# Value stage of an expert feed-forward: six sums kept in their PSUM banks over all 128 blocks instead of being added out every four blocks

## The reference, cut to what matters

```
def per_head(hargs):
    e, g = hargs
    act = jax.nn.gelu(jnp.einsum('ld,lkd->lk', xb, u_tab[e]), approximate=False)
    return jnp.einsum('lk,lkd->ld', act * g, v_tab[e])
...
    y = peer_ffn(h, peer_wq[l], peer_keys[l], peer_u[l], peer_v[l])
    h = layer_norm(DEEPNORM_ALPHA * h + y, ln2_g[l], ln2_b[l])
```

## Time and profile before

| What | us |
| --- | --- |
| median of three runs | 2871.51 (2864.45 to 2873.06) |
| the profiled execution's own time | 2873.07 |
| its span, first to last instruction | 2871.3 |
| first `ex_gated_hi` to last `ex_gated_hi` of the value stage | 582.12 |
| last `ex_gated_hi` to the first instruction of the layer norm | 19.31 |
| mean granted TensorE clock over the span | 0.949 of full |

### The profile page before, as it was taken

How to read it: one execution, slowest core, us unless ns; L and a number is a source line. 1 busy time by engine, 2 the same in 40 slices (tenths; PEclk the granted TensorE clock), 3 DMA queues, 4 the chain that set the end, 5 groups by cost and what they waited for, 6 DMA issues and landing times. The chain is left out here.

```text
span 2871.3 us, 43150 instructions
## 1 busy us (share of the span) xinstructions
PE 2503.2 (87%) x14285; PEld 1409.1 (49%) x14285; DVE 1771.6 (62%) x3539; ACT 900.6 (31%) x1357; POOL 1232.4 (43%) x744
## 2 busy tenths in 40 slices
PE   5999998967999999988989899978888698888885
PEld 3344343435677766675434455545555233333332
DVE  6123122027676666753331798889997688888886
ACT  4212212123323333222223333334443233333332
POOL 3312313213122122212323577666565576777764
PEclk9999999988999999999989999999999899999998
DMA  5201201121000000002231588768989899999994
GB/s 184 88 29 58 88 29 66 52 84 45 8 29 22 29 29 29 7 0 85 78 126 49 166 266 285 246 223 314 350 325 354 280 310 310 315 317 316 315 312 144
DMA packets 192978, 456.84 MB, mean 159 GB/s; under 512 B 17664, under 2 KB 100224, under 8 KB 192784
## 3 DMA queue, kind: packets, MB, share of 16 engines
q1 hardware_dynamic: 149136, 296.59, 29.6%
q0 software_dynamic: 36864, 134.23, 14.6%
q10 hardware_dynamic: 6912, 25.17, 2.2%
HBM read 403.50 MB, written 52.43 MB: 159 GB/s over the span
## 5 line engine op out<-in xcount | busy, mean ns | idle before, releaser
L1760 POOL TENSOR_TENSOR hid_u_lo<-hid_u,hid_u_hi 128x1024 bf16<-128x1024 f32 x128 | 292.9, 2289 | 228.8 <-ACT hid_u_hi L1744 228.4
L2373 PE MATMUL bank<-ex_v_hi,ex_gated_hi 128*128 128x512 bf16 x768 | 301.4, 392 | 85.4 <-DVE ex_gated_lo L2431 73.4
L148 PE MATMUL bank<-hT_hi,hid_u_hi 128*128 128x384 bf16 x1024 | 337.6, 330 | 39.2 <-POOL hid_u_lo L1760 28.3
L2411 POOL TENSOR_TENSOR ex_v_lo<-ex_v,ex_v_hi 128x1024 bf16<-128x1024 f32 x128 | 274.3, 2143 | 153.8 <-ACT ex_v_hi L2395 153.7
L148 PE MATMUL bank<-hT_lo,hid_u_hi 128*128 128x384 bf16 x1024 | 337.2, 329 | 0.0
L148 PE MATMUL bank<-hT_hi,hid_u_lo 128*128 128x384 bf16 x1024 | 336.9, 329 | 0.0
L203 POOL TENSOR_TENSOR ret_w_lo<-ret_w_raw,ret_w_hi 128x1024 bf16<-128x1024 f32 x72 | 153.0, 2162 | 401.4 <-ACT ret_w_hi L198 401.4
L2373 PE MATMUL bank<-ex_v_hi,ex_gated_lo 128*128 128x512 bf16 x768 | 300.3, 391 | 0.0
L2373 PE MATMUL bank<-ex_v_lo,ex_gated_hi 128*128 128x512 bf16 x768 | 299.3, 390 | 0.0
L2438 DVE SCALAR_TENSOR_TENSOR wide<-ex_row,row_gated,wide 128x1024 f32<-128x1024 f32 x128 | 164.4, 1284 | 17.2 <-DMA ex_row<-in_peer_v,row_index 16.9
L2397 ACT ACTIVATE ex_gated_hi<-ex_gated 128x384 bf16<-128x384 f32 x128 | 66.9, 522 | 343.0 <-DVE ex_gated L2428 343.0
(11 more groups left out here) (486 smaller groups left out, 5785.7 us busy)
## 6 DMA issues: line engine op xcount, KB each, us to landing
hid_u<-in_peer_u SPq DMA_DIRECT2D x128, 512.0 KB, 5.5
ex_v<-in_peer_v SPq DMA_DIRECT2D x128, 512.0 KB, 6.1
ret_w_raw<-in_w_ret SPq DMA_DIRECT2D x60, 512.0 KB, 4.2
expert_hidden<-hid_gelu SPq DMA_DIRECT2D x128, 192.0 KB, 4.5
expert_weights<-spread_grid ACTq DMA_DIRECT2D x48, 512.0 KB
ex_gated<-expert_hidden SPq DMA_DIRECT2D x128, 192.0 KB, 4.6
ex_weights<-expert_weights SPq DMA_DIRECT2D x64, 384.0 KB, 5.8
dn_w_raw<-in_w_dn SPq DMA_DIRECT2D x36, 512.0 KB, 3.3
```

The source lines that it names most:

```text
L148: last = nc.tensor.matmul(out, left[l], right[r], start=start and i == 0, stop=stop and i == len(PASSES) - 1)
L1760: self.nc.gpsimd.tensor_tensor(self.us[1][:, m % 2, :, :], self.u32[:, m % RING, :, :], self.us[0][:, m % 2, :, :], ALU.subtract).then_inc ...
L2373: last = nc.tensor.matmul(bank[:, :], gs[l][:, slot, t * P:(t + 1) * P], vs[r][:, slot, half * 512:(half + 1) * 512], start=j == 0 and i == 0,
L2411: nc.gpsimd.tensor_tensor(vs[1][:, n % 8, :], v32[:, n % RING, :], vs[0][:, n % 8, :], ALU.subtract).then_inc(s["v_lo"], 1)
```

## The change: what it does

The groups go. Each of the six units has its bank for the whole stage: PE takes block after block, all six units of a block with three matmuls each, and adds up in the banks from block 0 (`start`) to block 127 (`stop`). DVE no longer adds out of PSUM inside the stage. At the end it does one operation per unit that scales `h` by ALPHA and adds the bank, so the six scalings ahead of the stage go too. The bf16 halves keep eight slots, now a plain ring: ACT waits before `ex_v_hi` of block n until PE is through with block n - 8 (`used`). Loads, gathers, the products, the splits and the row additions are unchanged, in the same order on their engines.

```
-            for j in range(GROUP):
-                step(j, j, None)
-            with eng.Fori(0, (BLOCKS - 2 * GROUP) // (2 * GROUP)) as turn:
-                for j in range(2 * GROUP):
-                    step(turn * (2 * GROUP) + (GROUP + j), GROUP + j, turn * 2 + j // GROUP)
...
+            for n in range(SLOTS):
+                step(n, n)
+            with eng.Fori(0, (BLOCKS - 2 * SLOTS) // SLOTS) as turn:
+                for j in range(SLOTS):
+                    step(turn * SLOTS + (SLOTS + j), SLOTS + j)
+            for n in range(BLOCKS - SLOTS, BLOCKS):
+                step(n, n)
...
             @block.tensor
             def _(pe):
-                def units(n, m, group):
-
-                    side = (m // GROUP - 1) % 2
-                    for u in units_of(m):
...
-                        pe.wait_ge(s["added"], group * UNITS + (u + 1))
-                        for j in range(GROUP):
-                            slot = GROUP * side + j
-                            for i, (l, r) in enumerate(PASSES):
...
+                def step(n, m):
+                    first, last_one = isinstance(n, int) and n == 0, isinstance(n, int) and n == BLOCKS - 1
+                    slot = m % SLOTS
+                    for name in ("gated_hi", "gated_lo", "v_hi", "v_lo"):
+                        pe.wait_ge(s[name], n + 1)
+                    for u, (half, t) in enumerate(UNITS):
+                        for i, (l, r) in enumerate(PASSES):
+                            last = nc.tensor.matmul(core.banks[u][:, :], gs[l][:, slot, t * P:(t + 1) * P],
+                                                    vs[r][:, slot, half * 512:(half + 1) * 512],
+                                                    start=first and i == 0, stop=last_one and i == 2)
+                        if last_one:
+                            last.then_inc(s["summed"], 1)
+                    if not last_one:
+                        last.then_inc(s["used"], 1)
...
             @block.scalar
...
-                    if m >= GROUP:
-
-                        act.wait_ge(s["added"], group * UNITS + UNITS)
+                    if m >= SLOTS:
+
+                        act.wait_ge(s["used"], n - (SLOTS - 1))
...
             @block.vector
             def _(dve):
-                def add_units(n, m, group):
-                    for u in units_of(m):
-                        half, t = divmod(u, TILES_IN)
-                        dve.wait_ge(s["unit"], group * UNITS + (u + 1))
-                        part = acc[:, t, half * 512:(half + 1) * 512]
-                        nc.vector.tensor_tensor(part, part, core.banks[u][:, :], ALU.add)\
-                            .then_inc(s["added"], 1)
...
-                    if m >= GROUP:
-                        add_units(n, m, group)
...
-                for u in range(UNITS):
-                    half, t = divmod(u, TILES_IN)
-                    part = acc[:, t, half * 512:(half + 1) * 512]
-                    nc.vector.tensor_scalar(part, part, ALPHA, None, ALU.mult).then_inc(s["added"], 1)
-                dve.wait_ge(s["added"], UNITS)
-                run(dve, step, add_units)
+                run(dve, step)
+                for u, (half, t) in enumerate(UNITS):
+                    dve.wait_ge(s["summed"], u + 1)
+                    part = acc[:, t, half * 512:(half + 1) * 512]
+                    nc.vector.scalar_tensor_tensor(out=part, in0=part, scalar=ALPHA, in1=core.banks[u][:, :],
+                                                   op0=ALU.mult, op1=ALU.add)
```

More of the change, by code:

```diff
@@ L2313, in experts @@
     TILES_IN = DENSE // P
-    UNITS = 2 * TILES_IN
+    UNITS = [(half, t) for t in range(TILES_IN) for half in range(2)]
+    SLOTS = 8
     with ExitStack() as ctx:
@@ L2317, in experts @@
         v_in, wt_in, hid_in = (incoming.arrived[name] for name in ("v", "weights", "hidden"))
-        vs = [sbuf(nc, ctx, f"ex_v_{n}", [P, 2 * GROUP, D], BF16) for n in ("hi", "lo")]
-        gs = [sbuf(nc, ctx, f"ex_gated_{n}", [P, 2 * GROUP, DENSE], BF16) for n in ("hi", "lo")]
+        vs = [sbuf(nc, ctx, f"ex_v_{n}", [P, SLOTS, D], BF16) for n in ("hi", "lo")]
+        gs = [sbuf(nc, ctx, f"ex_gated_{n}", [P, SLOTS, DENSE], BF16) for n in ("hi", "lo")]
         row = sbuf(nc, ctx, "ex_row", [P, RING, D])
@@ L2322, in experts, with run @@
         own = core.wide
-        names = "v_hi v_lo gated gated_hi gated_lo unit added row_added".split()
+        names = "v_hi v_lo gated gated_hi gated_lo used row_added summed".split()
         s = {n: core.sem("ex_" + n) for n in names}
         rows_dram = incoming.dram["v"].rearrange("a b d -> (a b) d")
-        def units_of(m):
-            return range(UNITS * (m % GROUP) // GROUP, UNITS * (m % GROUP + 1) // GROUP)
-        def run(eng, step, last_units):
-            for j in range(GROUP):
-                step(j, j, None)
-            with eng.Fori(0, (BLOCKS - 2 * GROUP) // (2 * GROUP)) as turn:
-                for j in range(2 * GROUP):
-                    step(turn * (2 * GROUP) + (GROUP + j), GROUP + j, turn * 2 + j // GROUP)
[L2337 to L2340, removed]
+        def run(eng, step):
+            for n in range(SLOTS):
[5 more added lines that the diff above has]
+                step(n, n)
         def arrived(n, m):
@@ L2361, in _ @@
             def _(pe):
-                def units(n, m, group):
-                    side = (m // GROUP - 1) % 2
-                    for u in units_of(m):
-                        half, t = divmod(u, TILES_IN)
-                        bank = core.banks[u]
-                        pe.wait_ge(s["added"], group * UNITS + (u + 1))
-                        for j in range(GROUP):
-                            slot = GROUP * side + j
-                            for i, (l, r) in enumerate(PASSES):
[L2373 to L2377, removed]
@@ L2379, in step @@
-                def step(n, m, group):
-                    if m >= GROUP:
[L2381 to L2386, removed]
+                def step(n, m):
[12 more added lines that the diff above has]
+                        last.then_inc(s["used"], 1)
@@ L2388, in _, with step @@
+                run(pe, step)
             @block.scalar
             def _(act):
-                def step(n, m, group):
+                def step(n, m):
                     act.wait_ge(v_in[m % RING], arrived(n, m))
-                    if m >= GROUP:
-                        act.wait_ge(s["added"], group * UNITS + UNITS)
-                    nc.scalar.activation(vs[0][:, m % 8, :], v32[:, m % RING, :], ACT.Copy).then_inc(s["v_hi"], 1)
+                    if m >= SLOTS:
+                        act.wait_ge(s["used"], n - (SLOTS - 1))
+                    nc.scalar.activation(vs[0][:, m % SLOTS, :], v32[:, m % RING, :], ACT.Copy)\
+                        .then_inc(s["v_hi"], 1)
@@ L2396, in step @@
                     act.wait_ge(s["gated"], n + 1)
-                    nc.scalar.activation(gs[0][:, m % 8, :], g32[:, m % RING, :], ACT.Copy)\
+                    nc.scalar.activation(gs[0][:, m % SLOTS, :], g32[:, m % RING, :], ACT.Copy)\
                         .then_inc(s["gated_hi"], 1)
-                run(act, step, lambda n, m, group: None)
+                run(act, step)
             @block.gpsimd
```

8 lines of the change are left out of this document (2 added, 6 removed).

## The result

The changed kernel takes 2808.59 us (median of four runs, 2803.96 to 2812.80), the kernel before 2869.11 in the same comparison; the ratio is 0.9786, 95% interval 0.9774 to 0.9798. The forecast was 2809, in a range of 2796 to 2846.

The account below looks back on a forecast made before the run. Bound: a 4.12 us loop of ex_gated_hi, ex_v_hi, ex_v_lo and product over ACT, POOL and DVE, plus ACT's wait every fourth block. 48.7 + 11.4 + 2.0 = 62.1 off 2873.07, less 1.56, gives 2809 us; range 2796 to 2846.

Parts of the forecast that it names:

- What bounds the kernel: Value stage: a loop of ex_gated_hi, ex_v_hi, ex_v_lo and product over three engines, 4.12 us; every fourth block about 6.05.
- Item 1: Stage: ACT's wait for added goes; 127 intervals at 4.12 us make 523.2, 58.9 less; the wait's own row says 54.6.
- Item 2: Stage on DVE: the 192 additions go, worth nothing by themselves, but the row addition comes forward by 0.6 or 1.2 us.
- one of the forecast's signs: Row addition: DVE's waits for ex_row were to total well over 16.9 us if the forecast was right.
- Item 3: Stage: gathers landing late become the next limit, 4.20 us per block instead of 4.12, so 533.4 us, 48.7 less.
- the formula with a single landing: Gather loop over three blocks: landing L + 5.66 us, a third per block; L taken as 6.95 gives 4.20.
- the forecast's sign of a median landing of 6.5 or more: Gathers in the stage: a median landing of 6.5 us or more was to show the forecast right.
- Item 4: DMA engines in the stage, as a check: 1.442 MB per block at 345 GB/s is 4.18 us, nearly filling the interval.
- Rival C: Stage: transfers become the bound, landings 7.6 to 8.2, 4.42 to 4.62 us per block, kernel 2841 to 2863 us; chance 17%.
- Items 5 and 6: End: one block left before the layer norm, 11.4 us less. Start: six scalings go from before the first product, 2.0 less.
- Item 7: PE in the stage: bank changes every 3 matmuls and a wait per block cost zero, at most 0.05 us per block.
- rival D: PE in the stage: TensorE falls to 1.2 GHz and the kernel gets slower, 3013 us at half the matmuls; chance 5%.

Follow-up runs that it names:

- e6: Changed kernel with gathers issued one block earlier and GpSimd subtracting only 512 of 1024 columns of ex_v_lo, PE using that half twice: 2769.51 us, ratio 0.9654.
- e12: Changed kernel with gathers one block earlier and the subtraction shared, GpSimd 512 columns, VectorE the other 512 in its idle time: 2772.95 us, ratio 0.9661.
- e3: Kernel before with twelve slots instead of eight for the bf16 halves, so ACT's wait for additions never binds; additions stay: 2824.85 us, ratio 0.9844.
- e1: Changed kernel with GpSimd issuing each gather one block earlier, before its subtraction of the preceding block: 2801.86 us, ratio 0.9756.
- e2: Changed kernel with each gather issued one block later, behind the subtraction of its own block: 2984.57 us, ratio 1.0393.
- e11: Changed kernel with four slots for the bf16 halves instead of eight: 2811.16 us, ratio 0.9799.
- e8: Kernel before with GpSimd's gathers issued one block earlier and nothing else changed: 2861.77 us, ratio 0.9972.
- e9: Changed kernel with gathers one block earlier and GpSimd's subtraction split into two instructions of 512 columns: 2794.64 us, ratio 0.9738.

## Why the prediction was right, step by step

- What bounds the kernel: right, and shown. The 4.12 us loop over ACT, POOL and DVE holds after the change (104 intervals), and shortening POOL's part opens it (e6, e12). That the product is held by POOL and not by its own data is shown by e6 and e12: the products that begin beside none of POOL's shorter subtractions run in 0.56 (every second block), those that begin during one in 1.1 to 1.2.
- Item 1, the wait of ACT: right. e3 removes it alone and the stage falls by 48.8.
- Item 2, the additions worth nothing in themselves: right in the stage, by e3. The row addition did come forward, and its waits went from 16.9 to 83.2 us. But that is not what made the rows late: with the additions in place (e3) the stage takes the same 4.20 per block, so the total of these waits, one of the forecast's signs, says little of the cost.
- Item 3, the late gather: right in mechanism, lucky in size. Late gathers put 4.19 in place of 4.12; e1 takes that back, and e2 makes it worse by the amount that the loop over two blocks gives. The free limit, 6.7 us from issue to row addition, was 6.8. But the formula with a single landing does not give the 4.19: with the median of 6.2 it gives (6.2 + 5.66) / 3 = 3.95, no loss at all, and the 4.20 came from a landing of 6.95 taken for every block. In fact 102 of the 127 intervals were at 4.11 to 4.14 and 25 paid 0.35 us each on average. The landing was over-estimated, the formula left the spread out, and the two errors met; the forecast's sign of a median landing of 6.5 or more did not come.
- Item 4, the check by the DMA engines: the step that failed. 4.18 from 345 GB/s agreed with the 4.2 by chance: e1 carries 350 and e6 and e12 383 GB/s, 3.77 us per block. A packet-time share of 1.0 was read as full, and it went to 1.06. Rival C did not come: it wanted landings of 7.6 to 8.2, and the median was 6.2. Landings of 7.7 (e6) and 7.9 (e12) came at 383 GB/s and with the gathers a block ahead, where rows that late cost nothing; what they would cost with the gathers in their old place no run shows.
- Items 5 and 6: 11.7 and 1.4 against 11.4 and 2.0, both within their bounds. At the start the product began early and was held until POOL's first subtraction had ended; the 2.0 was a guess between 0 and 4.7, and e11 shows that the start goes otherwise in another execution.
- Item 7 and rival D: bank changes every three matmuls and a wait per block did not lower the clock; the granted clock was 1.00 through 400 us with PE idle 4% of it.
- What I had not seen: rows that come late already cost the kernel before some 8 us (e8), through 0.36 us per group.

## What to carry to other kernels

When no engine is full, follow one block through the timeline until it closes on itself, and look which waits are in that loop. Here 192 additions, 125 us of VectorE, were worth nothing by themselves, and one wait, 54.6 us in total, was worth nearly the whole gain in the stage. Before removing a wait, compute from the issue and landing times how late the next input may be, with the number of blocks over which its own loop closes, and use the spread of the landings and not one value. Issuing the gather one block earlier took a few lines and ended its lateness. Where one engine's operation holds up another's, a part of it moved into an idle slot of the other engine shortens the loop: e12 gained 29.8 us over e1, until PE was the bound.

## What the runs showed of the hardware that was not expected

- The sixteen DMA engines moved 383 GB/s for 400 us (e6 and e12) with transfers of 512-byte to 4-KB pieces, at a summed packet share of 1.06; a share of 0.9 to 1.0 was no bound. The price was latency, 9.6 us for 512 KB instead of 6.1, and at this rate every second product waited for its load.
- VectorE's product, held by a GpSimd subtraction, was let in between two back-to-back subtractions when it came 0.67 us after the first began, and not when it came 0.26 after (e9). One that began 0.06 us ahead of a subtraction ran free in 0.55 and held the subtraction for 0.35 (e8); the first product of the changed kernel began 0.62 ahead and was held all the same.
- VectorE does 128 x 512 of the subtraction in 0.68 us (e12), GpSimd in 1.16; whole, GpSimd takes 2.13.
